# Order of the V row and the U row in each pair of gathers

## The chip, the cores and the metric

The kernel runs on one core of a Trainium2 chip. The metric is the time of one execution on the device in microseconds. The kernel before the change took 2286.2 us as the median of 3 runs (2282.84 to 2289.01). "Row" below means one gathered tile of 128 table rows, one for each of 128 tokens.

## The reference

One layer with 256 tokens of width 2048: an adaLN modulation, a token mixer (attention beside a gated recurrence), a layer norm, and then the PEER channel mixer, in which the change lies. For each token and each of 8 heads, PEER scores two halves of a query against 128 keys each, takes the 16 best of the sums, and treats each choice as the number of a single-neuron expert out of 128 x 128:

```python
cand = (s_top[:, :, 0, :, None] + s_top[:, :, 1, None, :]).reshape(n_tok, PEER_HEADS, -1)
best, pos = lax.top_k(cand, PEER_TOPK)
expert_idx = jnp.take_along_axis(cand_idx, pos, axis=-1)
gates = jax.nn.softmax(best, axis=-1)
act = jnp.einsum('td,thkd->thk', xb, u_tab[ib])
w = gb * jax.nn.gelu(act, approximate=False)
out = jnp.einsum('thk,thkd->td', w, v_tab[ib])
```

So each of the 256 x 8 x 16 choices needs one row of the table U (an inner product with the token) and one row of the table V (added to the token's output with the weight w). A second layer norm ends the layer.

## The kernel before

The tokens are two blocks of 128. The gathered part of PEER runs over n = 0 to 15, which is block n // 8 and head n % 8 (the text calls each n a head), and over e = 0 to 15, the choices. U(n,e) is the gather of the U rows of choice e in head n for 128 tokens, V(n,e) the gather of the V rows. Each is one indirect DMA of GpSimd (L489, in `gather_row`). An index of 12288 or more (the last 32 of 128 groups of experts) is out of bounds and moves nothing; those experts are computed densely with tiles that SyncE loads (`dense_u`, L441, and the end of the V table, L444).

There are five slots for U rows and five for V rows; row number 16n + e goes to slot (16n + e) % 5. Slots 0 to 3 lie in the tile `arena` and slot 4 in `mod_rows`, so that every fifth gather of a table shows `mod_rows` in the profile. Before each gather GpSimd waits alone (L343) until the slot is free: `u_used`, counted up by VectorE's reduction, or `v_used`, counted up by TensorE. GpSimd works through one written order and stands still at any of these waits.

- VectorE: `reduce_row(n, e)` (L1410) waits for U(n,e), multiplies it with the tokens and sums. After `reduce_row(n, 0)` it does `weigh(n - 1)` (L1417, L1421), which needs ScalarE's `gelu(n - 1)` and makes the weights of head n - 1. In heads 0 to 4 the choice of the experts (top-k, L1335 to L1387) is woven between the reductions; `s_ex` tells GpSimd that a head's experts are there. In heads 5 to 8 the masks for the dense experts are.
- ScalarE: `gelu(n)` (L653, 16 small activations) starts after the reduction of U(n,15).
- TensorE: `weigh_row(n, e)` (L974, 4 matmuls) adds V(n,e) with its weights. Head n - 1 is weighed in turn n of the loop, and the matmuls of the dense experts (L1002, L1014) and of the gates (L1040) stand between the rows. The first eight rows of head 0 are weighed among the query projections (L1048). After the last V row of each group of choices the output is normalised and stored.

GpSimd's order (L506 to L523): the U rows of head 0, with V(0,0) to V(0,4) among the last of them; then for n from 1 to 15 and e from 0 to 15 the pair U(n,e), V(n-1,e); last the sixteen V rows of head 15. Head 1 differs: its pairs are U(1,e), V(0,e+1) for e from 4 to 14, and its other U rows stand alone. At n = 2, 5 and 9 GpSimd also waits (`s_exq`) for the expert numbers in the layout of the V rows.

Of the kernel before, what the change touches and what calls it, by code (L numbers as in the profile page):

```python
# [143 lines left out]
def block_kernel(nc, consts, x_rows, x_t, cond_cols, ada_early, ada_late, bias_cols, bias_late, w_early, weights, lb_logits, norm_gain,  # L144
                 ln_rows, subkeys_t, expert_u, expert_v, dense_u, x_mid, out):
    with ExitStack() as ctx:
# [193 lines left out]
        def wait_alone(engine, sem, value):  # L340

            engine.wait_ge(sem, value)
            engine.nop(nofuse=True)  # L343
# [117 lines left out]
        @block.gpsimd  # L461
        def _(pool):
            for x in from_one:
                pool.sem_inc(x, 1)
            nc.gpsimd.memset(one_col, 1.0).then_inc(s_ones, 1)
            nc.gpsimd.memset(mod_rows[:], 0.0).then_inc(s_zero, 1)
            pool.wait_ge(s_zero, 1)
            pool.dma_start(mod_rows[0:1, :], bias_late).then_inc(s_bias, 16)
            pool.wait_ge(early_used[0], 1 + EARLY_STEPS // 2)
            pool.wait_ge(s_first_mod, 1)  # L470

            for g in range(2):
                with pool.Fori(0, KT // 2) as i:
                    for s in range(2):
                        pool.wait_ge(ada_used[s], i + (1 + g * KT // 2))
                        pool.dma_start(ada_slot[s], ada_late[ds((i * 2 + s) * P, P), g * ADA_COLS:(g + 1) * ADA_COLS])\  # L476
                            .then_inc(ada_loaded[s], 16)
            for s in range(2):
                pool.wait_ge(ada_used[s], 1 + KT)
            pool.dma_start(ln1, ln_rows[0:2, :].partition_broadcast(P)).then_inc(s_ln[0], 16)  # L480


            def gather_row(table, indices, n, e, slots, row_used, row_loaded):

                row = n * TOPK + e
                ring = len(slots)
                wait_alone(pool, row_used[row % ring], 1 + row // ring)
                column = n % HEADS * TOPK + e
                pool.indirect_dma_start(slots[row % ring], None, table,  # L489
                                        bass.IndirectOffsetOnAxis(ap=indices[:, n // HEADS, column:column + 1], axis=0),  # L490
                                        bounds_check=GATHERED - 1, oob_is_err=False)\
                    .then_inc(row_loaded[row % ring], 16)

            def gather_u(n, e):
                gather_row(expert_u, expert, n, e, u_slot, u_used, u_loaded)

            def gather_v(n, e):
                gather_row(expert_v, expert_q, n, e, v_slot, v_used, v_loaded)


            for b in range(BLOCKS):
                pool.wait_ge(s_x1, b + 1)
                pool.dma_start(x_mid[b * P:(b + 1) * P, :], xr[:, b]).then_inc(s_mid, 16)
            wait_alone(pool, s_ex, 1)
            for e in range(TOPK):
                gather_u(0, e)  # L506
                early = e - (TOPK - 2 * V_RING + 1)
                if early == 0:
                    wait_alone(pool, s_exq, 1)
                if early >= 0 and early % 2 == 0:  # L510
                    gather_v(0, early // 2)
            for n in range(1, BLOCKS * HEADS):
                wait_alone(pool, s_ex, n + 1)
                for e in range(TOPK):
                    gather_u(n, e)
                    if e == 0 and n in (2, 5, HEADS + 1):
                        wait_alone(pool, s_exq, (2, 5, HEADS + 1).index(n) + 2)
                    if n > 1:
                        gather_v(n - 1, e)
                    elif V_RING <= e + 1 < TOPK:  # L520
                        gather_v(0, e + 1)
            for e in range(TOPK):
                gather_v(BLOCKS * HEADS - 1, e)  # L523

        @block.scalar
        def _(act_e):
# [139 lines left out]
            def experts_to_quads(i):  # L666

                b, _, end = BATCHES_OF_HEADS[i]
                act_e.wait_ge(s_ex, b * HEADS + end)
                batch_to_quads(expert_q, expert, i).then_inc(s_exq, 1)  # L670

            def gates_to_quads(i):

                b, _, end = BATCHES_OF_HEADS[i]
                act_e.wait_ge(s_gl, b * HEADS + end)
                batch_to_quads(gates_q, gates_left, i).then_inc(s_gq, 1)
# [942 lines left out]
```

## Time and profile before

| | us |
|---|---|
| median of 3 runs | 2286.2 |
| the profiled execution | 2278.52 |
| its span, first to last instruction | 2276.9 |
| TensorE busy | 1937.7 (85%) |
| VectorE busy | 1365.1 (60%) |
| GpSimd busy | 782.8 (34%) |
| ScalarE busy | 390.6 (17%) |

The profile covers one execution. "Busy" counts instructions in work; a matmul's end is modelled. DMA share is the mean busy share of the core's 16 DMA engines. "Idle before <- releaser" names what ended the idle time of an engine ahead of an instruction; "issue" means that nothing in the profile shows what it was. The gathers run from 1035.7 us to 2254.5 us of the span.

### The profile page before, as it was taken

Reading aid. Unit: us, or ns where it says so; the run is one execution under the profiler, and the core shown is the slowest. Engines: PE = TensorE matmul, PEld = TensorE weight load, DVE = VectorE, ACT = ScalarE, POOL = GpSimd, SP = SyncE. Lnnn points to the kernel's source line nnn. Section 1 sums busy time; section 2 is a strip of 40 time slices with the busy share of each in tenths; the row PEclk is TensorE's granted clock in tenths of the full one; section 3 lists DMA queues with packets and bytes.
Section 4 is the critical chain, followed back from the end, with each engine's and each line's share of the span. In section 5 each row is a group of like instructions: output and inputs, shape, how many; then the busy total and the mean of one; then the engine's idle time right before and its main releaser. Section 6 shows DMA issues by size and latency. Waiting matters only on the chain.

```text
span 2276.9 us, 27806 instructions
## 1 busy us (share of the span) xinstructions
PE 1937.7 (85%) x10646; PEld 1309.3 (58%) x10646; DVE 1365.1 (60%) x2008; ACT 390.6 (17%) x1001; POOL 782.8 (34%) x554
## 2 busy tenths in 40 slices
PE   4899899998999999989888888888975888897455
PEld 4788688887888888878654545555640222221001
DVE  7821378776444441246798889777876444444664
ACT  0112212211000001021232212544530000000011
POOL 1000000000000000004365546767878644554783
PEclk9999899999999999999899899888985999999556
DMA  9963366575576656318899999999999999999997
GB/s 391 428 276 143 116 270 246 216 292 197 234 284 245 230 212 259 140 69 331 311 383 414 405 408 414 398 402 398 392 406 371 417 417 410 399 413 354 364 365 270
DMA packets 104603, 722.41 MB, mean 317 GB/s; under 512 B 29740, under 2 KB 29740, under 8 KB 32060
## 3 DMA queue, kind: packets, MB, share of 16 engines
q0 software_dynamic: 78800, 466.66, 51.9%
q1 hardware_dynamic: 25696, 254.35, 28.0%
q8 instruction: 65, 1.06, 0.2%
q14 instruction: 42, 0.34, 0.0%
HBM read 858.35 MB, written 4.19 MB: 379 GB/s over the span
## 4 chain that ended last, share of the span: by engine, by line
PE 43%; DMA 29%; DVE 12%; issue 8%; POOL 5%; ACT 2%; POOLq 0%; DVEq 0%; SPq 0%; ACTq 0%
PE ps L777 21%; DMA arena<-expert_u,expert 14%; DMA arena<-expert_v,expert_q 11%; PE ps L785 10%; POOL arena L489 4%; PE ps L801 3%; PE ps L974 3%; DVE work L1410 2%; PE ps L1002 2%; DMA mod_rows<-expert_u,expert 2%; DVE mod_rows L1167 1%; PE ps L1048 1%; DMA mod_rows<-expert_v,expert_q 1%; DVE work L1223 1%; DVE work L1130 1%
## 5 line engine op out<-in xcount | busy, mean ns | idle before, releaser
L1410 DVE CUSTOM_DVE_ANT_0 work<-arena,buf_b 128x2048 f32<-128x2048 f32 x166 | 380.8, 2294 | 265.5 <-DMA arena<-expert_u,expert 232.1
L974 PE MATMUL ps<-arena,mod_rows 128*32 128x512 f32 x1640 | 270.5, 740 | 197.1 <-DMA arena<-expert_v,expert_q 166.0
L777 PE MATMUL ps<-buf_a,arena 128*128 128x256 f32 x1920 | 424.2, 383 | 6.1 <-DVE arena L1241 5.3
L777 PEld LDWEIGHTS ps<-buf_a,arena 128*128 128x128 f32 x1920 | 367.5, 192 | 57.2 <-issue 6.7
L489 POOL DMA_INDIRECT arena<-expert_v,expert_q x205 | 339.8, 1658 | 159.1 <-PE ps L974 97.1
L489 POOL DMA_INDIRECT arena<-expert_u,expert x205 | 266.1, 1298 | 239.8 <-DVE work L1410 124.2
L476 POOL DMA_DIRECT2D arena<-ada_late x32 | 16.9, 529 | 770.9 <-DVE mod_rows L1167 642.7
L1002 PE MATMUL ps<-arena 128*128 128x256 f32 x1024 | 273.3, 418 | 4.2 <-DMA arena<-dense_u 4.2
L1002 PEld LDWEIGHTS ps<-arena 128*128 128x128 f32 x1024 | 202.8, 207 | 128.8 <-issue 94.8
L974 PEld LDWEIGHTS ps<-arena,mod_rows 128*32 128x32 f32 x1640 | 37.2, 118 | 333.2 <-DMA arena<-expert_v,expert_q 270.3
L653 ACT ACTIVATE work<-work 32x4 f32<-32x4 f32 (+3 forms) x320 | 66.4, 207 | 551.3 <-DVE work L1410 543.8
L1167 DVE SCALAR_TENSOR_TENSOR mod_rows<-arena,cols,mod_rows 128x4096 f32<-128x4096 f32 x32 | 143.4, 4482 | 3.2 <-DVE mod_rows L1167 1.1
L1410 DVE CUSTOM_DVE_ANT_0 work<-mod_rows,buf_b 128x2048 f32<-128x2048 f32 x42 | 96.4, 2294 | 57.1 <-DMA mod_rows<-expert_u,expert 50.3
L1014 PE MATMUL ps<-arena 128*32 128x512 f32 x1024 | 119.1, 606 | 0.1
L1014 PE MATMUL ps<-arena,buf_a 128*32 128x512 f32 x1024 | 117.6, 600 | 0.0
L1048 PE MATMUL ps<-arena 128*128 128x256 f32 x512 | 115.7, 386 | 0.8 <-ACT arena L625 0.8
L785 PE MATMUL ps<-arena,buf_a 128*128 128x256 f32 x512 | 112.4, 379 | 0.0
L777 PE MATMUL ps<-arena 128*128 128x256 f32 x512 | 111.8, 379 | 0.0
L785 PE MATMUL ps<-arena,buf_b 128*128 128x256 f32 x512 | 111.4, 379 | 0.0
L1048 PEld LDWEIGHTS ps<-arena 128*128 128x128 f32 x512 | 97.8, 193 | 19.2 <-issue 5.0
L1410 DVE CUSTOM_DVE_ANT_0 buf_a<-arena,buf_b 128x2048 f32<-128x2048 f32 x39 | 89.4, 2292 | 31.6 <-DMA arena<-expert_u,expert 31.0
L785 PEld LDWEIGHTS ps<-arena,buf_b 128*128 128x128 f32 x512 | 97.2, 190 | 15.7 <-issue 2.8
(244 smaller groups left out, 2083.1 us busy)
## 6 DMA issues: line engine op xcount, KB each, us to landing
arena<-weights SPq DMA_DIRECT2D x62, 2048.0 KB, 8.0
arena<-ada_late POOLq DMA_DIRECT2D x32, 2048.0 KB, 9.4
arena<-ada_early SPq DMA_DIRECT2D x16, 2048.0 KB, 17.7
arena<-dense_u SPq DMA_DIRECT2D x32, 1024.0 KB
arena<-expert_v SPq DMA_DIRECT2D x32, 1024.0 KB
arena<-w_early SPq DMA_DIRECT2D x8, 1536.0 KB, 9.8
arena<-expert_u,expert POOLq DMA_INDIRECT x205
arena<-expert_v,expert_q POOLq DMA_INDIRECT x205
```

The lines of the kernel that those rows point to most:

```text
L489: pool.indirect_dma_start(slots[row % ring], None, table, bass.IndirectOffsetOnAxis(ap=indices[:, n // HEADS, column:column + 1], axis=0), ...
L653: last = run(target(k, g), source(k, g), function)
L777: last = mm(ps[:, bank, c * TOKENS:(c + 1) * TOKENS], ring[slot][:, first + k, c * P:(c + 1) * P], rhs[:, k, :], start=(k == 0), stop=(k = ...
L785: last = mm(ps[:, bank, b * COLS:(b + 1) * COLS], lhs[:, k, b * P:(b + 1) * P], ring[slot][:, k, :], start=(k == 0), stop=(k == KT - 1))
L801: last = mm(ps[:, c // 2, c % 2 * TOKENS:(c % 2 + 1) * TOKENS], early_slot[g % 2][:, k, c * P:(c + 1) * P], h_t[:, 2 * g + k, :], start=fi ...
L974: last = mm(ps[j * GROUP:(j + 1) * GROUP, n // HEADS * QUADS + g, :], spread_w[n % 2][:, e, :], v_slot[row % V_RING][:, j * QCOLS:(j + 1) ...
L1002: last = mm(ps[:, 4 + a % 2, 0:TOKENS], tile[:, k, :], h2_t[:, k, :], start=k == 0, stop=k == KT - 1)
L1014: last = mm(ps[j * GROUP:(j + 1) * GROUP, r, :], dense_act[a // 16][:, a % 16, r * GROUP:(r + 1) * GROUP], dense_slot[t % 2][:, j * QCOLS: ...
L1048: last = mm(ps[:, 6 + s, i // 2 * TOKENS:(i // 2 + 1) * TOKENS], ring[s][:, k, i // 2 * P:(i // 2 + 1) * P], h2_t[:, k, :], start=k == 0, ...
L1130: row = v.scalar_tensor_tensor(out=total, in0=tile[:, r], scalar=factor, in1=total, op0=ALU.mult, op1=ALU.add)
L1167: v.scalar_tensor_tensor(out=sums, in0=ada_slot[s], scalar=cond[:, ds(k, 1)], in1=sums, op0=ALU.mult, op1=ALU.add).then_inc(ada_used[s], 1)
L1410: v.tensor_tensor_reduce(out=products[n > 2], in0=u_slot[s], in1=h2[:, n // HEADS], scale=1.0, scalar=0.0, op0=ALU.mult, op1=ALU.add, accu ...
```

## The change

From head 1 on the U gather of each pair is asked for after the V gather. The wait on `s_exq` at e = 0 of heads 2, 5 and 9 keeps its place ahead of the V gather, and so now stands ahead of U(n,0) as well. The waits of each gather go with it. Nothing else differs.

```diff
             for n in range(1, BLOCKS * HEADS):
                 wait_alone(pool, s_ex, n + 1)
                 for e in range(TOPK):
-                    gather_u(n, e)
                     if e == 0 and n in (2, 5, HEADS + 1):
                         wait_alone(pool, s_exq, (2, 5, HEADS + 1).index(n) + 2)
                     if n > 1:
                         gather_v(n - 1, e)
                     elif V_RING <= e + 1 < TOPK:
                         gather_v(0, e + 1)
+                    gather_u(n, e)
             for e in range(TOPK):
                 gather_v(BLOCKS * HEADS - 1, e)
```

## Rows read from the trace of the kernel before

**Rows 1.** The page: engines, busy share of the DMA engines, bytes of two queues, issues.

```profile
PE 1937.7 (85%) x10646; PEld 1309.3 (58%) x10646; DVE 1365.1 (60%) x2008; ACT 390.6 (17%) x1001; POOL 782.8 (34%) x554
...
DMA  9963366575576656318899999999999999999997
...
q0 software_dynamic: 78800, 466.66, 51.9%
...
arena<-ada_late POOLq DMA_DIRECT2D x32, 2048.0 KB, 9.4
```

**Rows 2.** The page: the chain that ended last, by engine.

```profile
PE 43%; DMA 29%; DVE 12%; issue 8%; POOL 5%; ACT 2%; POOLq 0%; DVEq 0%; SPq 0%; ACTq 0%
```

**Rows 3.** Windows: from:to, length, busy us and instructions, granted clock, DMA share, GB/s.

```profile
1105.00:1160.00 55.00, 45.06 (x232) 30.47 (x232) 46.80 (x121) 13.68 (x42) 28.31 (x23) 0.89 0.83 297
1170.00:1420.00 250.00, 210.09 (x1019) 126.70 (x1018) 221.03 (x557) 57.24 (x145) 140.16 (x104) 0.92 1.01 411
1420.00:1700.00 280.00, 239.51 (x1422) 158.77 (x1420) 207.01 (x339) 135.55 (x396) 212.43 (x130) 0.90 1.00 400
1711.50:1797.10 85.60, 58.44 (x396) 12.05 (x400) 48.07 (x44) 3.28 (x16) 72.16 (x45) 0.68 0.99 389
1800.00:2110.00 310.00, 256.96 (x2264) 69.38 (x2256) 138.62 (x125) 13.11 (x64) 149.86 (x116) 0.97 1.01 399
2116.50:2215.20 98.70, 51.40 (x220) 8.75 (x216) 70.10 (x76) 6.32 (x20) 84.12 (x47) 0.50 0.97 369
2231.00:2277.00 46.00, 27.84 (x144) 6.97 (x144) 18.97 (x43) 2.72 (x9) 11.02 (x11) 0.65 0.68 242
```

**Rows 4.** Timeline of GpSimd, head 1: start, length, tiles, idle before.

```profile
1111.38 0.99 POOL L489 DMA_INDIRECT arena<-expert_u,expert  x1 [0.30 <-issue]
1120.19 1.07 POOL L489 DMA_INDIRECT arena<-expert_v,expert_q  x1 [7.82 <-PE ps L974]
...
1159.44 2.41 POOL L489 DMA_INDIRECT mod_rows<-expert_u,expert  x1 [0.30 <-issue]
```

**Rows 5.** Timeline of VectorE, the reduction of U(1,13).

```profile
1172.81 2.29 DVE L1410 CUSTOM_DVE_ANT_0 buf_a<-mod_rows,buf_b 128x2048 f32<-128x2048 f32 x1 [0.21 <-DMA mod_rows<-expert_u,expert]
```

**Rows 6.** Timeline of GpSimd around the end of head 11.

```profile
1904.47 0.99 POOL L489 DMA_INDIRECT arena<-expert_u,expert  x1 [0.30 <-issue]
...
1935.32 1.23 POOL L489 DMA_INDIRECT arena<-expert_v,expert_q  x1 [0.97 <-PE ps L974]
```

**Rows 7.** The chain in order of time, U(11,15) from issue to landing.

```profile
1900.68 22.26 DMA arena<-expert_u,expert
```

**Rows 8.** Timelines of VectorE, U(12,0), and of TensorE, V(11,0).

```profile
1930.22 2.29 DVE L1410 CUSTOM_DVE_ANT_0 work<-arena,buf_b 128x2048 f32<-128x2048 f32 x1 [4.84 <-issue]
...
1933.39 1.06 PE L974 MATMUL ps<-arena,mod_rows 128*32 128x512 f32 x8 [2.19 <-DVE mod_rows L1421]
```

**Rows 9.** Timeline of GpSimd after U(14,15).

```profile
2148.63 0.99 POOL L489 DMA_INDIRECT mod_rows<-expert_u,expert  x1 [0.30 <-issue]
...
2172.68 3.02 POOL L489 DMA_INDIRECT arena<-expert_u,expert  x1 [0.30 <-issue]
2176.01 0.99 POOL L489 DMA_INDIRECT mod_rows<-expert_v,expert_q  x1 [0.30 <-issue]
```

**Rows 10.** Timeline of TensorE, V(14,0) and V(14,1).

```profile
2169.25 1.94 PE L974 MATMUL ps<-mod_rows 128*32 128x512 f32 x8 [3.57 <-DVE mod_rows L1421]
```

**Rows 11.** Timeline of GpSimd, U(15,15), V(14,15), V(15,5) and V(15,15).

```profile
2215.19 1.15 POOL L489 DMA_INDIRECT arena<-expert_u,expert  x1 [0.30 <-issue]
2216.65 3.01 POOL L489 DMA_INDIRECT mod_rows<-expert_v,expert_q  x1 [0.31 <-PE ps L974]
...
2234.36 0.98 POOL L489 DMA_INDIRECT arena<-expert_v,expert_q  x1 [3.62 <-PE ps L974]
...
2254.49 0.99 POOL L489 DMA_INDIRECT arena<-expert_v,expert_q  x1 [1.00 <-issue]
```

**Rows 12.** Timeline of VectorE, the last two lines of reductions that matter here.

```profile
2216.51 2.29 DVE L1410 CUSTOM_DVE_ANT_0 work<-arena,buf_b 128x2048 f32<-128x2048 f32 x1 [1.02 <-DMA arena<-expert_u,expert]
...
2224.58 2.29 DVE L1410 CUSTOM_DVE_ANT_0 work<-arena,buf_b 128x2048 f32<-128x2048 f32 x1 [0.29 <-DMA arena<-expert_u,expert]
```

**Rows 13.** Timeline of TensorE, V(15,0) on.

```profile
2231.55 6.06 PE L974 MATMUL ps<-arena,mod_rows 128*32 128x512 f32 x32 [2.66 <-DVE mod_rows L1421]
```

## Prediction

> **What bounds the kernel now.** The view to begin with is the page. By busy time TensorE looks like the bound, at 85% [rows 1], and the chain that ended last gives it 43% and DMA 29% [rows 2]. That is a mean over two halves. The line of DMA shares in the same group stands between 1 and 7 in most slices up to 1020 us and at 8 or 9 from then to the last slice, and the gathers run just there. So the windows come next, cut where the order of work changes [rows 3]. From 1170 to 2110 us the DMA engines are busy for 0.99 to 1.01 of the time at 389 to 411 GB/s; TensorE and VectorE have idle time in every one of these stretches. The second half of the kernel is a stream of transfers, and a change of order that leaves the bytes alone can only act where that stream thins out, or at its end.
>
> How much is one gather? The queue of GpSimd moved 466.66 MB [rows 1]. The 32 `ada_late` tiles of 2048 KB are 67.1 MB of it; the gains of the layer norm (2.1 MB) and the stored rows (2.1 MB) go off too, and 395.3 MB are left for 2 x 256 gathers: 0.772 MB each, since an out-of-bounds index moves nothing. At 400 GB/s that is 1.9 us.
>
> Two stretches differ. From 1711.5 to 1797.1 and from 2116.5 to 2215.2 us no dense tiles are loaded. They hold 45 and 47 gathers, both ends included [rows 3], so 44 and 46 intervals: 1.95 and 2.15 us for each place in GpSimd's order, with GpSimd busy for 84 and 85% of the time. Here GpSimd and the DMA engines are about equally the bound. From 2231 us on the DMA share is 0.68: the tail is a chain of latencies.
>
> **The change part by part.** No instruction is added or taken away: 512 gathers, the same waits, the same bytes. Written as one stream, the order before is U V U V and the order after is V U V U, and that is again an alternation. So inside the stream nothing alternates differently. What changes is one number: relative to the U rows, every V row from V(0,5) to V(14,15) is asked for one place sooner, and each U row one place later. I price that at the three kinds of place where it can be seen.
>
> *Start, head 1.* Before, U(1,4) goes out at 1111.38 and GpSimd then stands 7.82 us for V(0,5), until TensorE has weighed V(0,0) at 1120.19 [rows 4]. After, U(1,4) stands behind that wait and goes out at about 1121.5, and every U row of the stretch goes out when its successor did. The V rows keep their times, since TensorE paces them among the query projections. From 1105 to 1160 us the DMA share is 0.83 at 297 GB/s [rows 3], so a row missing here is a row of transfer not done, and the stream is full afterwards and never gives it back: +1.9 us. Does VectorE, busy for 46.8 of these 55 us, starve as well? U(1,13) was asked for at 1159.44 and landed just ahead of its reduction at 1172.81 after 0.21 us of idle time [rows 4, 5], so from there a U row one place later is also about 2 us late. These are the same 2 us, seen from another engine. Bounds: 0, if the idle share of the DMA engines takes the row in later, and 4, if it is lost on both. I take 1.9.
>
> *Ends of heads 1 to 14.* This is where a lookahead matters. V(n,0) can't be weighed until `weigh(n)`, which follows the reduction of U(n,15), 16 activations and the reduction of U(n+1,0). Meanwhile the V ring fills with V(n,0) to V(n,4), and V(n,5) stands before a full ring. Before, V(n,5) stands 13 places behind U(n,15); after, 11. In head 11: U(11,15) takes 22.26 us to land [rows 7]; U(12,0), asked for at 1904.47, is reduced at 1930.22; TensorE starts on V(11,0) at 1933.39 after 2.19 us of idle time [rows 6, 8]; and V(11,5) goes out at 1935.32, having waited 0.97 us for it [rows 6]. So the wait is there already. After the change U(12,0) lands a row later, the weights come some 2 us later, and V(11,5) and U(12,5) behind it go out 2 to 4 us later. Four U rows and four V rows are on their way by then, which at 1.9 us each is 15 us of transfer for the engines besides the dense tile: they don't run dry, and the cost is 0 while the queue is that deep. Eleven or so of these ends lie in such stretches. The two others lie where rows land in about 10 us. At 2169 us: V(14,5) went out at 2176.01, and its slot was free from about 2170.2 (the eight matmuls from 2169.25 are two rows in 1.94 us) [rows 9, 10], so 5.8 us to spare. After, V(14,5) takes the place of U(15,5) at 2172.68 [rows 9], and the slot comes free one place later, at 2172.4. The 5.8 us go to 0.3 but not below nothing: 0, up to 2 us for each of the two if I misjudge the place. I take 0.
>
> *End.* The last U row, U(15,15), goes out at 2215.19 and V(14,15) at 2216.65 behind it [rows 11]. After, they swap. U(15,15) is reduced from 2224.58, and seven us later TensorE starts on V(15,0) [rows 12, 13]; V(15,5) to V(15,15) go out from 2234.36 to 2254.49, each when a slot comes free [rows 11], and the rest of the chain hangs on them. So the tail, from 2231.55 to the end of the span at 2276.9, moves as a whole with the landing of U(15,15). One place later is 1.3 us if V(14,15) takes the short form (0.99 and 0.3 between gathers, as at 2148.63 [rows 9]) and 3.3 us in the long form (3.01 and 0.3); the mean place of the stretch is 2.15 us, and I take that. That V(14,15) lands earlier gains nothing, for it is weighed before `weigh(15)` in any case.
>
> The `s_exq` waits now stand ahead of U(2,0), U(5,0) and U(9,0). ScalarE fulfils them, and the view of waits lays none of GpSimd's idle time to ScalarE, so they were met before GpSimd came to them; one place sooner I price them at 0, up to 1 us each.
>
> *Sum.* 1.9 + 0 + 2.15 = 4.05 us on the profiled execution's 2278.52, so 2282.6. The median of the runs lies 7.7 us above the profiled one; I add the same difference to it: 2286.2 + 4.05 = 2290.3, rounded to 2290. The bounds together: 0 + 0 + 1.3 below, 4 + 4 + 3.3 + 3 above, so +1 to +14.
>
> **The rivals.**
>
> *The full V ring holds back U rows and the stream runs thin (slower).* The place is V(n,5) in each of heads 1 to 14, with U(n+1,5) now behind it and not ahead. It decides as soon as the wait there outlasts the rows under way. Each end then costs a place, 14 x 2.15 = 30 us, and the time is 2316. For it: the wait exists already (0.97 us), and the slack at 2176 shrinks to 0.3 us. Against it: a DMA share of 1.0 with landings of 22 us, which a thinner queue would shorten first. If it holds only where masks or few transfers leave the queue short, half of it: 2301. Chance 0.17.
>
> *The V gathers no longer collide with the reductions (faster).* Look at V(14,15): it starts at 2216.65, in the middle of the reduction that runs from 2216.51 to 2218.80, and takes 3.01 us, ending 0.86 us after the reduction; U(15,15), which starts outside one, takes 1.15 [rows 11, 12]. In the two gather-only stretches GpSimd loses the difference nearly once a pair, most often on V. Were the new phase such that the reduction falls into a wait, a pair would come down to what the DMA engines allow, 1.544 MB at the 411 GB/s of rows 3, or 3.76 us, in place of 3.89 and 4.29: 22 x 0.13 + 23 x 0.53 = 15 us, so 2275. Against it: the alternation is the same and the collision moves with the landings, whichever table's turn it is. Chance 0.12.
>
> The Trainium skill ("SBUF — State Buffer", "Who interferes with whom") has the rule behind this: VectorE with two SBUF inputs and GpSimd reading SBUF share a port pair under an exclusive lock, and whoever issues second is blocked wholly, so that issue order decides. The trace agrees with "blocked to the end of the reduction": the long gather ends 0.86 us after it, near a whole short gather of 0.99. By that rule alone an order of issue could matter, which is why this case has a chance of its own.
>
> *Everything is hidden (no change).* The missing row at the start is taken in by the idle shares of 1105 to 1160 us, and the end costs 1.3: 2287. Chance 0.13.
>
> **How the numbers follow.** The forecast, 2290 with a range of its own from 2286 to 2295, has 0.58; the slower rival 0.17, the faster 0.12, the hidden case 0.13. About 0.3%, or 6.9 us, is what a measurement of this kernel can tell from no change. Slower by more than that (over 2293.1): 0.16 from the first rival and 0.10 from the upper bounds of the forecast's terms, 0.26. Faster (below 2279.3): 0.10 of the faster rival and 0.02 from the scatter of the runs, 0.12. The rest is 0.62. The range for 8 in 10 is 2278 to 2304: it leaves out the full form of the first rival and most of the faster one.
>
> **What would show it.** In the changed kernel U(1,4) should go out behind V(0,5) after an idle time near 7.8 us. The DMA share should stay at 1.0 from 1170 us on. At the ends of heads, idle time of GpSimd ahead of V(n,5) should grow by 1 to 3 us, and TensorE's idle time ahead of V(n,0) by 2 to 5, with no loss in GB/s. U(15,15) should land about 4 us later in the span than 2224.5, and the stretch from there to the end should be 52 us as now. GB/s below 395 between 1170 and 2110, or idle GpSimd in the gather-only stretches, would speak for the slower rival; a pair shorter than 3.8 us there for the faster one. The prediction is wrong if the time moves by more than 7 us either way.

## The result and the profile after

The changed kernel took 2301.9 us as the median of 4 runs (2297.06 to 2303.41), beside 2284.5 for the kernel before (2281.99 to 2289.01). The ratio is 1.0071, with a 95% interval from 1.0055 to 1.0086: slower by 16 us (12.6 to 19.6). Its profiled span is 2295.4 us, 18.5 more than before. In this section times without a run named are of the two profiled executions.

The page of the changed kernel answers to [rows 1, 2]: busy times are the same within a few us, the DMA line looks the same, and 18.5 us have come in as idle time that no engine's total points to.

```profile
PE 1934.1 (84%) x10646; PEld 1312.1 (57%) x10646; DVE 1364.7 (59%) x2008; ACT 391.5 (17%) x1001; POOL 775.2 (34%) x554
...
DMA  9963366575575646418799999999999999999996
...
PE 45%; DMA 28%; DVE 10%; issue 9%; POOL 6%; ACT 1%; POOLq 0%; DVEq 0%; SPq 0%; ACTq 0%
```

The windows, with the cuts of [rows 3], tell more (length, busy us of TensorE, its weight loads, VectorE, ScalarE, GpSimd, granted clock, DMA share, GB/s). Changed kernel:

```profile
1105.00:1160.00 55.00, 45.00 (x232) 30.43 (x232) 46.46 (x113) 10.58 (x30) 25.26 (x20) 0.88 0.80 278
1170.00:1420.00 250.00, 206.22 (x1020) 125.30 (x1018) 219.94 (x559) 57.57 (x148) 146.00 (x105) 0.92 1.00 406
1420.00:1700.00 280.00, 236.63 (x1410) 157.53 (x1406) 204.99 (x338) 134.21 (x386) 195.59 (x126) 0.90 0.99 394
1800.00:2110.00 310.00, 269.20 (x2376) 74.00 (x2368) 136.03 (x122) 10.89 (x54) 155.64 (x121) 0.96 1.00 401
```

The head 1 stretch moves 278 GB/s and not 297. From 1170 to 1700 us the rate falls from 411 and 400 to 406 and 394, and the DMA share from 1.01 and 1.00 to 1.00 and 0.99. Both fall by a little over 1%, which the two digits of the share barely show.

Where GpSimd stands still is in the view of waits: engine, line, whom it waited for, us in total, times, the longest. From 1105 to 2235 us, the rows of the four slots in `arena` alone, first the kernel before, then the changed one:

```profile
POOL arena L489 <- PE ps L974: 128.8, 77, 7.8
POOL arena L489 <- DVE work L1410: 112.4, 37, 7.2
```

```profile
POOL arena L489 <- PE ps L974: 175.0, 75, 9.9
POOL arena L489 <- DVE work L1410: 82.6, 30, 5.0
```

The idle time has moved from U slots to V slots. I added up the idle time above 0.3 us ahead of each V gather, by e, over the timeline of heads 1 to 15: ahead of V(n,5), for n from 1 to 15, it was 20 us before and is 83 us now. No other e holds over 12. Of the 14 waits from V(1,5) to V(14,5), 12 grew, and their mean grew by 4.2 us.

At one end of a head it looks like this. GpSimd in the changed kernel, head 11 (start, length, tiles, idle before), to be read against [rows 6]:

```profile
1936.40 0.99 POOL L489 DMA_INDIRECT arena<-expert_u,expert  x1 [2.38 <-DVE work L1410]
1939.46 0.99 POOL L489 DMA_INDIRECT arena<-expert_v,expert_q  x1 [2.06 <-PE ps L974]
1943.86 0.99 POOL L489 DMA_INDIRECT arena<-expert_u,expert  x1 [3.42 <-issue]
1950.19 2.10 POOL L489 DMA_INDIRECT arena<-expert_v,expert_q  x1 [5.34 <-PE ps L974]
1952.59 0.99 POOL L489 DMA_INDIRECT arena<-expert_u,expert  x1 [0.30 <-issue]
```

The fourth line is V(11,5). It waited 5.34 us, where before it waited 0.97 [rows 6], and U(12,5) goes out behind it. Between 1939.46 and 1950.19 GpSimd asked for one row. TensorE and VectorE at the same place, to be read against [rows 8]:

```profile
1947.38 1.94 PE L974 MATMUL ps<-arena,mod_rows 128*32 128x512 f32 x8 [5.36 <-DVE mod_rows L1421]
```

```profile
1943.83 2.35 DVE L1410 CUSTOM_DVE_ANT_0 work<-arena,buf_b 128x2048 f32<-128x2048 f32 x1 [1.11 <-DMA arena<-expert_u,expert]
1946.42 0.18 DVE L1417 TENSOR_TENSOR work<-work 128x16 f32<-128x16 f32 x1 [0.23 <-ACT work L653]
```

And the stream itself, in windows of 10 us around the end of head 11; kernel before, then changed:

```profile
1920.00:1930.00 10.00, 8.15 (x76) 2.26 (x76) 3.02 (x4) 3.28 (x16) 3.95 (x4) 1.00 1.00 404
1930.00:1940.00 10.00, 7.82 (x76) 2.24 (x72) 6.51 (x7) 0.00 (x0) 3.59 (x4) 1.00 0.99 384
1940.00:1950.00 10.00, 10.00 (x100) 2.99 (x92) 3.76 (x5) 0.00 (x0) 7.50 (x5) 1.00 0.98 389
```

```profile
1940.00:1950.00 10.00, 4.64 (x36) 1.04 (x32) 6.39 (x7) 3.27 (x16) 1.44 (x2) 0.81 0.98 396
1950.00:1960.00 10.00, 10.00 (x84) 2.65 (x80) 6.03 (x6) 0.00 (x0) 6.36 (x4) 0.85 0.84 324
1960.00:1970.00 10.00, 10.00 (x100) 2.72 (x96) 3.38 (x3) 0.00 (x0) 5.98 (x6) 1.00 0.97 373
```

The stream thins to 324 GB/s. TensorE stands idle for 5.36 us, and the granted clock reads 0.81 and 0.85 in these windows. Two streams have thinned at once. The view of the DMA queues (packets, MB, share of 16 engines) has the gathers in q0 and SyncE's dense tiles in q1. Changed kernel, 1940 to 1950 us, then 1950 to 1960:

```profile
q0 software_dynamic: 557, 2.89, 71.4%
q1 hardware_dynamic: 139, 1.04, 25.9%
```

```profile
q0 software_dynamic: 600, 3.23, 83.5%
q1 hardware_dynamic: 5, 0.01, 0.2%
```

So in the thin window the gathers moved more than in the one before it, but they did not fill the place of the dense tile that was missing.

**Rows under way.** The trace also has the landings: each gather lands in 16 parts, and a row is under way here from the start of its gather to the last part. (In the trace of the kernel before, some parts are missing, so its counts are if anything too low.) When GpSimd comes to V(n,5), over the 14 ends, 7.2 rows are under way before and 7.4 in the changed kernel. When it gets past, 6.8 and 5.2. At V(11,5) in the changed kernel it is 8 rows, then 6, and 5 or 6 for the next 15 us, for then one row is asked for about as often as one lands. From 1170 to 1420 us, in steps of 5 us, the rate goes with that number:

| rows under way | before: steps, GB/s | changed | experiment 4 (below) |
|---|---|---|---|
| 6 and more | 50, 411 | 37, 416 | 33, 417 |
| 5 to 6 | none | 9, 386 | 4, 409 |
| 3 to 5 | none | 4, 356 | 8, 325 |
| under 3 | none | none | 5, 215 |

This is a count and not an experiment: the dense tiles run thin in the same steps, and how much of the loss is theirs is not separated. At the end of head 11 the kernel before has 384 and 389 GB/s with 7 to 9 rows under way, so the number is not the whole of it.

**The 18.5 us, by place.** The stream has 512 places in both kernels, so the end of the k-th gather can be compared with the k-th. At the end of head 0 the changed kernel is 3.5 us behind; nothing of the change has run by then, so this is scatter between two executions. At the end of head 1 it is 5.8 behind, a start term of 2.3. The place of the last pair began 14.9 later (V(14,15) at 2230.12, against U(15,15) at 2215.19 [rows 11]): 9.1 us more, made in heads 2 to 15. The weights of head 15 come 19.4 us later (U(15,15) below): an end term of 4.5. The end of the span is 18.5 later. The split is of one trace each and no finer than about 2 us: one place beyond the end of head 1 the changed kernel is 4.0 behind, not 5.8. Where the loss is made can also be read from the bytes moved: what the kernel before had moved by 1160, 1700 and 2100 us, the changed one has moved 5.3, 12.6 and 17.3 us later.

```profile
2230.12 0.99 POOL L489 DMA_INDIRECT mod_rows<-expert_v,expert_q  x1 [0.31 <-issue]
2231.41 2.76 POOL L489 DMA_INDIRECT arena<-expert_u,expert  x1 [0.30 <-issue]
```

```profile
2244.02 2.29 DVE L1410 CUSTOM_DVE_ANT_0 work<-arena,buf_b 128x2048 f32<-128x2048 f32 x1 [1.52 <-DMA arena<-expert_u,expert]
...
2250.24 0.69 DVE L1421 TENSOR_TENSOR mod_rows<-cst,work 128x512 f32<-128x512 f32 x1
```

### The profile page after: what moved, and what is told of

It is laid out like the page before. It is cut to its first block, busy times and chain, and to the rows that moved or that the text cites. A ratio compares the mean times of both kernels' runs of the same rounds, so it can differ in the third digit from the quotient of the medians.

```text
span 2295.4 us, 27806 instructions
## 1 busy us (share of the span) xinstructions
PE 1934.1 (84%) x10646; PEld 1312.1 (57%) x10646; DVE 1364.7 (59%) x2008; ACT 391.5 (17%) x1001; POOL 775.2 (34%) x554
## 4 chain that ended last, share of the span: by engine, by line
PE 45%; DMA 28%; DVE 10%; issue 9%; POOL 6%; ACT 1%; POOLq 0%; DVEq 0%; SPq 0%; ACTq 0%
PE ps L777 21%; DMA arena<-expert_u,expert 18%; PE ps L785 10%; POOL arena L489 5%; DMA arena<-expert_v,expert_q 4%; DMA mod_rows<-expert_u,expert 3%; PE ps L801 3%; PE ps L974 3%; PE ps L1014 3%; DVE mod_rows L1167 1%; PE ps L1048 1%; PE ps L1002 1%; DVE work L1223 1%; POOL mod_rows L489 1%; DVE work L1130 1%
## 5 line engine op out<-in xcount | busy, mean ns | idle before, releaser
L974 PE MATMUL ps<-arena,mod_rows 128*32 128x512 f32 x1640 | 265.1, 727 | 182.2 <-DMA arena<-expert_v,expert_q 101.5
L489 POOL DMA_INDIRECT arena<-expert_v,expert_q x205 | 307.6, 1500 | 227.8 <-PE ps L974 173.8
L489 POOL DMA_INDIRECT arena<-expert_u,expert x205 | 295.5, 1441 | 195.7 <-DVE work L1410 93.0
## 6 DMA issues: line engine op xcount, KB each, us to landing
arena<-ada_early SPq DMA_DIRECT2D x16, 2048.0 KB, 17.4
```

The costliest lines, as they stand in the source:

```text
L489: pool.indirect_dma_start(slots[row % ring], None, table, bass.IndirectOffsetOnAxis(ap=indices[:, n // HEADS, column:column + 1], axis=0), ...
L974: last = mm(ps[j * GROUP:(j + 1) * GROUP, n // HEADS * QUADS + g, :], spread_w[n % 2][:, e, :], v_slot[row % V_RING][:, j * QCOLS:(j + 1) ...
```

## The experiments

Theory A puts the cost at the ends of heads, B at the start and end of the stream, C in every swapped pair. All ratios are to the kernel before, which ran beside each set of experiments on the same chip, in 5 rounds. The diffs are cut, and are against the kernel before unless the text says otherwise. In them `v_first` stands for the order of the change (V, then U).

**1. One pair of each head.**

```diff
-                    gather_u(n, e)
+                    v_first = n > 1 and e == 5
+                    if not v_first:
+                        gather_u(n, e)
...
+                    if v_first:
+                        gather_u(n, e)
```

> The order of before, with V first in one pair of each head only: e = 5, heads 2 to 15. Every other gather keeps its place. Theory A (the change costs time because V(n,5), which meets a full V ring, now stands ahead of U(n+1,5) and holds it back, while the eight rows issued before it land): most of what the change costs comes back here, 5 to 12 us over before, and GpSimd's idle time ahead of the V gathers of e = 5 grows from 20 us towards 50. Theory B (start and end of the stream carry the cost): 0. Theory C (what counts is the whole stream's shift, through collisions of gathers with reductions): at most 1 us, since 14 of 240 pairs are swapped.

Measured: 1.0019 (1.0007 to 1.0030), 2288.2 us, 4.3 us over before. The idle time ahead of V(n,5) went to 55 us. So U(n+1,5) behind a waiting V(n,5) does cost something, but it is a quarter of the change's cost and below the 5 us that A in this narrow form said at least, though 34 of the change's 62 us of added idle time ahead of V(n,5) are there. Idle time there is no measure of the cost by itself.

**2. All pairs but that one.** As 1, with `v_first = not (n > 1 and e == 5)`.

> The changed kernel, with U first again in the one pair e = 5 of heads 2 to 15. V(n,5) is 12 places behind U(n,15), between the 13 of before and the 11 of the change. Theory A: 4 to 9 us over before, about half of the cost gone. Theory B: as the changed kernel, 14 to 18 us over before. Theory C: as the changed kernel too.

Measured: 1.0062 (1.0043 to 1.0080), 14 us. The narrow form of A falls: idle time ahead of V(n,5) was down to 34 us, but 32 us stood ahead of V(n,6), in front of U(n+1,6). The wait only moved to the next pair. What is left is the wide form of A: the cost is made around the ends of heads, whichever pair waits.

**3. Start and end alone.** As 1, with `v_first = n in (1, BLOCKS * HEADS - 1)`.

> V first in heads 1 and 15 only, so the start, the last full V ring but one (head 14) and the end have the new order and nothing between. The prediction's terms for start and end say 4 us over before (1.9 and 2.15). Theory A: 3 to 5, one thirteenth of the ends of heads and the two end terms. Theory B: the whole cost, 14 to 18 us.

Measured: 1.0012 (1.0000 to 1.0024), 2.7 us. B falls as the main cause: start, end and the end of head 14 together cost 0 to 5.5 us. By place, its trace stands 4.0 us further behind at the end of head 1 than at the end of head 0, stands 3 to 7 us behind at the ends of heads 2 to 14, and gains 4.5 in the last 16 places.

**4. Another place for the V rows.**

```diff
-                    gather_u(n, e)
...
-                        gather_v(n - 1, e)
...
+                    gather_v(n - 1 + (e + 1) // TOPK, (e + 1) % TOPK)
+                    gather_u(n, e)
```

The waits on `s_exq` move with the V rows, and V(1,0) goes out ahead of U(1,15).

> One more place in the same direction: V(n-1,e+1) is asked for before U(n,e), so V(n,5) stands 9 places behind U(n,15) (before 13, changed kernel 11). Theory A: the wait at the full ring grows by another two places each time and the rows under way are two fewer, so the cost grows by more than it did, 35 to 60 us over before. Theory B: the start and the end shift by two more places, about 8 us more than the changed kernel, 22 to 26 over before. Theory C: within 5 us of the changed kernel, because the alternation is the same again.

Measured: 1.0268 (1.0248 to 1.0287), 2343.6 us, 61 us: at the upper edge of A's 35 to 60, and far outside B and C. V(n,5) stands 9 places behind U(n,15), and the idle time ahead of it is 142 us. GpSimd around V(10,5), and the windows there:

```profile
1882.93 0.99 POOL L489 DMA_INDIRECT mod_rows<-expert_u,expert  x1 [3.41 <-DVE work L1416]
1896.38 1.20 POOL L489 DMA_INDIRECT arena<-expert_v,expert_q  x1 [12.46 <-PE ps L980]
```

```profile
1880.00:1890.00 10.00, 1.10 (x12) 0.13 (x4) 4.39 (x4) 3.15 (x16) 0.99 (x1) 0.77 1.01 417
1890.00:1900.00 10.00, 6.42 (x36) 1.60 (x40) 7.68 (x8) 0.13 (x1) 3.31 (x2) 0.55 0.65 248
1900.00:1910.00 10.00, 10.00 (x96) 2.76 (x92) 4.60 (x4) 0.00 (x0) 5.99 (x5) 1.00 0.84 303
```

After 12.46 us without a request the stream runs at 248 GB/s. Most of the dip comes late in the wait and behind it: at 1885 us 8 rows are still under way, at 1895 us 4, and at 1905 us 2. At 11 of the 14 ends a window of 10 us holds between 162 and 313 GB/s.

**5. The middle of heads.** As 1, with `v_first = n > 1 and 7 <= e < 15`.

> V first only in the middle of heads 2 to 15, e = 7 to 14 (112 pairs); the pairs around each end keep the order of before, so V(n,5) stays 13 places behind U(n,15). Theory A, in the wide form that the first runs leave (the cost is made around the ends of heads, by V rows that fill a ring which can't be used yet while U rows wait behind them): 0, at most 2 us over before. Theory C (each swapped pair costs by itself, or the alternation with the reductions changes): 7 to 9 us, half of the cost for half of the pairs.

Measured: 1.0035 (1.0022 to 1.0049), 8.0 us. A said 2 at most and missed; C's figure is met. V(n,7), which here goes out right behind V(n,6), had 21 us of idle time ahead of it, and V(n,11) and V(n,12) together 27, against 6 and 12 before. So a V row asked for early waits in the middle of a head as well, if less. Part of this belongs to the experiment: in the changed kernel, where the order doesn't turn at e = 7, V(n,7) has 7 us.

**6. The ends of heads.** As 1, with `v_first = n > 1 and (e < 7 or e == 15)`.

> The other half: V first at e = 15 and e = 0 to 6 of heads 2 to 15 (112 pairs), U first in the middle. V(n,5) is 11 places behind U(n,15), as in the changed kernel, and U(n+1,5) and U(n+1,6) stand behind full-ring waits. Theory A in the wide form: all of the cost but what head 1 has, 12 to 16 us over before. Theory C: 7 to 9 us.

Measured: 1.0066 (1.0053 to 1.0079), 15.1 us. A is right here and C wrong: with the same number of swapped pairs as 5 it costs 7 us more. With 8.0 for the other half the halves don't add up to 16. Both orders turn round twice in each head, and at one of the turns a V row stands right behind a V row: here V(n,15), with 27 us of idle time ahead of it, against 2 before and 5 in the changed kernel. So each half has a cost of its own that the change doesn't have. An estimate from the three times: if it is the same in both, what is left adds up, and head 1 has 2 of the 16 us, then it is about 4.5 us each, the ends stand for some 10.5 of the 16 (the end term of the stream among them) and the middle for 3.5.

**7. and 8. Weights made ahead of the reduction of U(n+1,0),** in the changed kernel and in the kernel before.

```diff
+                    if n and e == 0:
+                        weigh(n - 1)
                     reduce_row(n, e)
...
-                    if n and e == 0:
-                        weigh(n - 1)
```

> The changed kernel, with VectorE making the weights of head n ahead of the reduction of U(n+1,0), not behind it, so that the full V ring waits for ScalarE's gelu only. Theory A: the ring opens sooner where U(n+1,0) lands late. In the changed kernel's trace of head 11 the gelu ended 0.23 us before the weights began, so little is to be had there; over all heads 3 to 8 us less than the changed kernel, that is 8 to 13 over before. If the cost did not hang on the time of the weights (B or C) the time stays at 14 to 18 over before.

> The kernel before, with the same move on VectorE. In head 11 the reduction of U(12,0) ended 3.4 us behind the gelu, so the weights and V(11,5) could come 3 us sooner, and V(n,5) goes out 2 to 3 us behind the weights in 14 of the 15 ends of the trace before. Theory A: 2 to 8 us below before. If the ends are harmless with 13 places, as the prediction had it: no change.

Measured: 1.0063 (1.0050 to 1.0075) and 1.0014 (1.0005 to 1.0024). In the changed kernel that is 14.4 us over before where A said 8 to 13: 1.8 us less than without the move, which the intervals can't tell from nothing. In the kernel before it is 3.2 us slower, against the expectation of 2 to 8 us faster, although the idle time ahead of V(n,5) fell from 20 to 5 us. Both traces say why there is little to win: VectorE now stands for the gelu (54 us in the 16 heads, where it stood 4 or 5 ahead of the weights without the move) and starts the reduction of U(n+1,0) 2.3 us later on the mean. Over 14 ends of the changed kernel the weights were ready 8.4 us behind the start of the reduction of U(n,15), and with the move 6.9.

**9. The other direction.**

```diff
-                    gather_u(n, e)
+                        gather_u(n + (e + 1) // TOPK, (e + 1) % TOPK)
...
-                        gather_v(n - 1, e)
...
+                    gather_v(n - 1, e)
```

> The other direction from the kernel before: U(n,e+1) is asked for before V(n-1,e) in heads 2 to 15 (head 1 as before), so V(n,5) stands 15 places behind U(n,15) (13 before, 11 in the changed kernel, 9 in the one that cost 61 us). Theory A in the wide form: GpSimd's idle time ahead of V(n,5), 20 us in all before, falls to a few us, and the time is 0 to 6 us below before; the U ring's own limit (U(k+5) behind the reduction of U(k)) then holds it. Theory C: 4 us or more over before or below it with no change of that idle time.

Measured: 1.0008 (0.9996 to 1.0019), no difference. The idle time ahead of V(n,5) fell from 20 to 3 us as A said, but the 0 to 6 us of gain did not come (its interval ends at 0.9 us below before). Rows under way are 7.3 at both ends of that wait, so there was little thinning to take away. No order that was tried beats the kernel before.

**10. and 11. Six V slots and four U slots,** in the changed kernel and in the kernel before.

```diff
-U_RING, V_RING = 5, 5
+U_RING, V_RING = 4, 6
...
-        u_slot = [arena[:, s * row:(s + 1) * row] for s in (4, 5, 6, 7)] + [shift2]
-        v_slot = [arena[:, s * row:(s + 1) * row] for s in (8, 9, 10, 11)] + [scale2]
+        u_slot = [arena[:, s * row:(s + 1) * row] for s in (4, 5, 6)] + [shift2]
+        v_slot = [arena[:, s * row:(s + 1) * row] for s in (7, 8, 9, 10, 11)] + [scale2]
```

> The changed kernel with one slot of the U ring given to the V ring: 4 U slots and 6 V slots. If the cost is that five V slots are too few ahead of the weights (narrow form of A), V(n,5) no longer stops, V(n,6) does, 13 places behind U(n,15) as V(n,5) did before, and the time is 0 to 5 us over before. If it is that too few rows which can still be used are under way at the end of a head (wide form), U(n+1,4) now stops 10 places behind U(n,15) for the reduction of U(n+1,0), and the time is 20 to 60 us over before.

> The kernel before with 4 U slots and 6 V slots. Narrow form of A: 0 to 3 us below before, as V(n,5) had little idle time there. Wide form: U(n+1,4) stops 10 places behind U(n,15) here too, so 15 to 50 us over before, and close to the changed kernel with the same slots.

Measured: 1.0080 (1.0060 to 1.0100), 18 us, and 1.0046 (1.0028 to 1.0065), 10.5 us. No idle time was left ahead of V(n,5), and the changed order was as slow as with five. Waits of GpSimd in the changed kernel with these slots, 1105 to 2235 us:

```profile
POOL arena L489 <- DVE work L1410: 230.7, 68, 6.7
POOL arena L489 <- PE ps L974: 17.8, 14, 4.1
```

The waits are now for U slots. So a V ring of five that fills up is not the whole cause: with ten slots in all, what one table gains the other lacks. With these slots the swap of U and V costs 7.5 us (about 2 to 14), where with five and five it costs 16, so the number of V slots may still have a part in it. The wide form had the direction right and the size wrong in both (20 to 60 and 15 to 50 expected).

**12. A short gelu** (the output's numbers are others, as the expectation says).

```diff
-                to_quads(lambda k, g: ...
...
+                run(gel_q, act[n % 2], ACT.Gelu).then_inc(s_gel, 1)
```

> The changed kernel with ScalarE's gelu of a head as one activation of 128 x 16 in place of 16 small ones. It leaves out the regrouping of the activations by quads of partitions, so the weights hold other numbers; every wait, gather and matmul stays. The weights come about 3.4 us sooner at each of 16 ends (3.65 us for the 16 small ones, about 0.2 for one). Theory A in the wide form (at the end of a head time runs from U(n,15) over the weights to V(n,5), and too little is under way meanwhile): at least half of the changed kernel's cost goes, so 0 to 9 us over before. If the end of a head is not what costs: 13 to 18 over before, less the 3.4 us of the last end.

Measured: 1.0071 (1.0059 to 1.0084), as the changed kernel. A said 0 to 9 us, and 16 came; the expectation rested on a false step. ScalarE's gelu of head 11, and VectorE's reduction of U(12,0) and weights in this trace:

```profile
1944.71 0.22 ACT L646 ACTIVATE work<-work 128x16 f32<-128x16 f32 x1 [86.45 <-DVE work L1409]
```

```profile
1945.77 2.37 DVE L1409 CUSTOM_DVE_ANT_0 work<-arena,buf_b 128x2048 f32<-128x2048 f32 x1 [1.10 <-DMA arena<-expert_u,expert]
...
1948.07 0.17 DVE L1416 TENSOR_TENSOR work<-work 128x16 f32<-128x16 f32 x1
```

The gelu was over at 1944.93, and the weights still began at 1948.07, behind the reduction of U(12,0). They wait for the later of two things, and each experiment took away one. So the run leaves the theory where it was: the weights were begun no sooner (on the mean of 14 ends 7.5 us behind the start of the reduction of U(n,15), as in the changed kernel), and nothing was tested. Both at once was not run.

## Why the prediction was right in its range and missed in its middle

The time, 2301.9, lies inside 2278 to 2304, at its upper edge. The range had been widened for the rivals. The forecast's own terms ended at +14 us, and the change cost 16. The likeliest case (no measurable change, 0.62) did not come, and by its own last sentence, which allowed 7 us either way, the prediction was wrong.

What came is the mechanism of the first rival, which had 0.17. That its half form said 2301 is luck. The half stood for half of the ends at 2.15 us each, but the wait grew at 12 of 14 ends and each cost about 1 us or less. And 2301, like 2316, leaves out the 4 us for start and end that the forecast itself counts; with them it is 2305, outside the range.

- *Start, +1.9.* Right as far as it can be told: 2.3 in the two profiled executions (0.5 one place further on), 4.0 in the trace of experiment 3, in a range of 0 to 4. U(1,4) did go out behind V(0,5).
- *Ends of heads, 0 "while the queue is that deep".* This is the step that failed. The count was right: four U and four V rows were "on their way" when GpSimd came to V(11,5), in the changed trace as well, 15 us of transfer by its sum. The wait was judged too short: 1 to 3 us more was the sign given, and the mean is 4.2. And the queue was taken to be either deep, at no cost, or dry. But it need not run dry to cost: with 5 to 6 rows under way the rate is 386 GB/s, with 3 to 5 it is 356, against 416 with six and more. In the changed trace a row's 16 parts land over 9.9 us on the mean (1170 to 2110 us), so a row that counts as under way has in part landed. That this is why the rate falls so early is a reading that no run tests. The term is 9.1 us by place in the two traces. By the runs it is about 13, the 16 of the change less the 2.7 of experiment 3. Experiment 6, with the change at the ends alone, costs 15.1 (12.1 to 18.0), where the start has the old order; the turns and the end term are in it.
- *"A DMA share of 1.0 with landings of 22 us, which a thinner queue would shorten first."* It did shorten them, and it cost time nonetheless. From a gather's start to its last part the mean of the rows of heads 1 to 14 is 17.4 us before and 16.5 after for U, 18.2 and 16.5 for V. (U(n,15) is asked for ahead of the wait and doesn't show it: 18.3 us from its gather to its reduction before, 19.0 after.) A mean hides the dips of 10 to 20 us, and so does the share: it reads 0.98 in a window with 396 GB/s and 0.97 in one with 373.
- *End, +2.15 out of 1.3 to 3.3.* Mis-sized by the two traces: 4.5. U(15,15) took the long form, 2.76 us, and its reduction began 12.6 us after it was asked for and not 9.4. The runs of experiment 3 are milder: start and end together, with the end of head 14, cost 2.7 us (0.0 to 5.5), where the forecast had 4.05.
- *The lock.* The gather that meets a reduction changed from V to U (V mean 1658 to 1500 ns, U mean 1298 to 1441 ns), and GpSimd's busy time went from 782.8 to 775.2 us. As predicted, the collisions move with the alternation and win nothing: 175 gathers began inside a reduction before and 184 after. The mean lengths of those in `arena` are in the two pages, first before, then changed.

```profile
L489 POOL DMA_INDIRECT arena<-expert_v,expert_q x205 | 339.8, 1658 | 159.1 <-PE ps L974 97.1
L489 POOL DMA_INDIRECT arena<-expert_u,expert x205 | 266.1, 1298 | 239.8 <-DVE work L1410 124.2
```

```profile
L489 POOL DMA_INDIRECT arena<-expert_v,expert_q x205 | 307.6, 1500 | 227.8 <-PE ps L974 173.8
L489 POOL DMA_INDIRECT arena<-expert_u,expert x205 | 295.5, 1441 | 195.7 <-DVE work L1410 93.0
```

**What is shown.** The cost grows with the lead of the V rows once it goes beyond that of the kernel before, and faster than the lead. The columns are the places from U(n,15) to V(n,5), the idle time ahead of V(n,5) over 15 heads, the rows under way when that wait ends (mean of 14), and the ratio:

| places | idle, us | rows under way | ratio |
|---|---|---|---|
| 15 (experiment 9) | 3 | 7.3 | 1.0008 |
| 13 (before) | 20 | 6.8 | 1 |
| 11 (changed) | 83 | 5.2 | 1.0071 |
| 9 (experiment 4) | 142 | 2.9 | 1.0268 |

It is made more around the ends of heads than in their middle (experiments 5 and 6), little of it at start and end (3), and one pair alone is not its cause (1, 2). The reading that fits all of these is that GpSimd stands before a V slot that can't come free until the weights are there, that the rows which it could ask for stand behind that wait, and that the rows under way meanwhile land and aren't replaced.

**What is open.** How the loss divides between gathers and dense tiles that come late. Whether rows under way are the cause or go along with it: no experiment changed their number with the order left alone; more slots in all would do it. What the turns in experiments 5 and 6 cost. Whether weights that come several us sooner would take the cost away: only 1.5 us was reached.

## What to carry to other kernels

When two streams share a queue and a set of slots, an order that alternates the same is not the same: find the place where one stream's rows can't be consumed yet, and count the rows under way at the end of the wait there, not at its start. At the start both kernels had seven. Don't price a thinner queue at nothing because it isn't dry. At the end of head 11 a wait of 1 us was there already; two places fewer made it 5 us, and four places fewer made it 12. To see whether a stream of transfers has thinned, read GB/s in windows of 10 us beside the busy share.

## What was unexpected of the hardware

- The DMA share and the rate come apart: 396 GB/s at a share of 0.98, 373 at 0.97, 324 at 0.84 and 248 at 0.65, while most full windows of the changed kernel show 415 to 421 GB/s at 1.01 to 1.02. Near the end of the dense tiles it is more: from 2100 to 2110 us the changed kernel has a share of 1.04 at 295 GB/s, and the kernel before from 2080 to 2090 us 1.03 at 287. The traces were not searched for the reason.
- The rate falls long before the queue is empty: in the changed kernel it was 386 GB/s with 5 to 6 gathers of 0.77 MB under way and 416 with six and more, though the dense tiles ran thin in the same steps.
- The cost of a stall in requests is not proportional to it. From before to the changed kernel 62 us more of idle time ahead of V(n,5) cost 16 us; from there to experiment 4 another 59 us cost 45.
